# Delta-rule phase of a hybrid layer: a key copy ahead of a weight cast, two weight low halves ahead of a cell expansion, and four more projection parts before the solver's first products

## The reference

```python
u = rmsnorm(h, norm_w)
proj = einsum('btd,dc->btc', u, w_in)          # four HGRN2 kinds, four delta-rule kinds, gates
# HGRN2, 4 heads: q, forget gate f, input i, output gate z; chunked causal scan
# Gated DeltaNet, 4 heads, per chunk of tokens:
A   = beta[..., None] * einsum('bhtd,bhsd->bhts', k, k) * dec_strict
lhs = eye(C) + A
sol = triangular_solve(lhs, concat([beta * v, beta * exp(gam) * k], -1), lower=True)
u_  = sol[..., :dv] - sol[..., dv:] @ S
o   = (q * exp(gam)) @ S + (einsum('bhtd,bhsd->bhts', q, k) * dec_incl) @ u_
S   = exp(g_last) * S + (k * exp(g_last - gam)).T @ u_
out = rmsnorm(h + concat([y_hg, y_gd], -1) @ w_out, final_norm_w)[:, 16:]
```

## Time and profile before

| | us |
|---|---|
| median of three runs | 833.71 (833.3 to 834.06) |
| the profiled execution | 836.43 |
| its span from first to last instruction | 834.7 |
| PE busy in it | 730.5 (88%) |
| DVE, POOL, ACT busy | 459.0, 347.9, 313.6 |

### The profile page before, as it was taken

The page is one execution under the profiler, slowest core; times in us unless marked ns, Lnnn a source line. Parts: engine busy times, 40 slices in busy tenths (PEclk is TensorE's granted clock), DMA queues, the critical chain, the costliest instruction groups (busy, mean ns, idle before and its releaser), DMA issues. The chain is left out here.

```text
span 834.7 us, 13559 instructions
## 1 busy us (share of the span) xinstructions
PE 730.5 (88%) x4803; PEld 687.6 (82%) x4803; DVE 459.0 (55%) x1011; ACT 313.6 (38%) x788; POOL 347.9 (42%) x455
## 2 busy tenths in 40 slices
PE   3398579989999998999998999999899968999985
PEld 3377579988899998989998989899899856888764
DVE  5625333525888244478862534989335164865146
ACT  4422383144454322533543244444431322332123
POOL 3626213134655342166543231658241335845125
PEclk9599789999999999999999999999999987999989
DMA  8410604242121425580636251202252133211004
GB/s 218 51 15 3 104 8 45 44 58 26 26 35 34 56 35 67 30 49 4 39 55 47 50 65 22 31 14 37 49 131 27 59 121 120 89 45 46 0 27 201
DMA packets 77030, 45.52 MB, mean 55 GB/s; under 512 B 30894, under 2 KB 72212, under 8 KB 76964
## 3 DMA queue, kind: packets, MB, share of 16 engines
q1 hardware_dynamic: 76964, 44.66, 31.9%
HBM read 36.41 MB, written 8.24 MB: 53 GB/s over the span
## 5 line engine op out<-in xcount | busy, mean ns | idle before, releaser
L221 PE MATMUL proj<-uTh,w_high 128*128 128x352 f32 (+1 forms) x768 | 265.9, 346 | 28.6 <-ACT hg_z L264 8.9
L221 PE MATMUL proj<-uTh,w_low 128*128 128x352 f32 (+1 forms) x768 | 249.2, 324 | 0.0
L221 PE MATMUL proj<-uTl,w_high 128*128 128x352 f32 (+1 forms) x768 | 248.9, 324 | 0.0
L221 PEld LDWEIGHTS proj<-uTh,w_high 128*128 128x128 f32 x768 | 147.6, 192 | 31.5 <-issue 15.2
L221 PEld LDWEIGHTS proj<-uTl,w_high 128*128 128x128 f32 x768 | 147.7, 192 | 0.0
L221 PEld LDWEIGHTS proj<-uTh,w_low 128*128 128x128 f32 x768 | 146.8, 191 | 0.0
L239 POOL TENSOR_TENSOR w_low<-w_raw,w_high 128x256 fp32r<-128x256 f32 (+1 forms) x57 | 77.9, 1366 | 48.6 <-ACT w_high L231 48.6
L1537 PE MATMUL mix<-level_x 128*128 128x128 f32 x448 | 66.0, 281 | 8.8 <-POOL level_x L1171 3.4
L1537 PEld LDWEIGHTS mix<-level_x 128*128 128x128 f32 x448 | 61.4, 194 | 13.9 <-issue 12.5
L1179 POOL TENSOR_TENSOR f_suffix<-f_suffix,f_prefix 128x192 f32<-128x192 f32 x84 | 56.2, 669 | 22.2 <-DVE f_prefix L1366 13.8
L1376 DVE COPY_PREDICATED hg_scores<-mask_st,mix 128x384 f32<-128x384 uint8 (+1 forms) x96 | 52.0, 542 | 18.2 <-PE mix L1537 18.0
(11 more groups left out here) (310 smaller groups left out, 1390.7 us busy)
## 6 DMA issues: line engine op xcount, KB each, us to landing
w_raw<-in_w_in SPq DMA_DIRECT2D x32, 512.0 KB, 8.5
x_tile<-in_x SPq DMA_DIRECT2D x8, 512.0 KB, 8.4
w_raw<-y_scratch SPq DMA_DIRECT2D x8, 384.0 KB, 3.8
decay<-gamma_scratch SPq DMA_DIRECT2D x4, 576.0 KB, 4.2
landing<-in_w_out SPq DMA_DIRECT2D x4, 512.0 KB, 8.0
landing<-in_x SPq DMA_DIRECT2D x3, 512.0 KB, 3.3
y_scratch<-gd_y SPq DMA_DIRECT2D x6, 192.0 KB, 1.8
decay<-in_w_out SPq DMA_DIRECT2D x2, 512.0 KB, 3.8
```

Of the source, the lines that this page charges most:

```text
L221: last = pe.matmul(acc[:, 0:tw], w[j % 2][:, k, :], u[:, k, t0:t0 + tw], start=(k == 0 and i == 0), stop=(k == KT - 1 and i == 2))
```

## The change

Three edits in `phase_gd`, for all heads.

```diff
-        give(("blocks", 1), 28)
+        give(("blocks", 1), 32)
...
                 for key in order:
+                    take_low(pool, parts[key])
                     if key == ("blocks", 1):
                         pool.wait_ge(m_in, 16)
                         expand(pool, M, blk_m).then_inc(m_set, 1)
-                    take_low(pool, parts[key])
...
-                    if (s, g) == ("A1", 1):
+                    if (s, g) == ("A2", 0):
                         split_high(act, 1)
                     take_hg(act, parts[(s, g)])
```

## The result

The changed kernel takes 859.02 us (median of four runs, 855.32 to 862.47) against 833.65 us before: a ratio of 1.0307, 95% interval 1.0281 to 1.0333. That is 25.4 us slower. The direction was forecast, and so was what makes PE wait (M behind tile 4, then the lower clock); the size was not, 18.4 us, and 859.02 lies just above the stated range of 843 to 859. The profiled execution took 862.47 us with a span of 860.7, so its rows show 26.0 us more than those of before.

A forecast was written before the change was run, and what follows sets the result against it. PE was taken to bound the kernel, busy 730.5 of 834.7 us. Z later 17.2, less 7.6 behind Z, plus 8.8 for the clock makes 18.4; 833.7 + 18.4 = 852.1, called 852, range 843 to 859.

The forecast's parts named there:

- Tile 4 in the chain of M: Before Z, POOL expands M only after tile 4's load, cast and low half; Z 17.2 us later over four heads.
- the signs that were named: Expansion behind tile 4's low half; PE waits 4 to 8 us before Z; three old waits gone; clock below 1.00 behind Z.
- the end of the waits for N: In the solver before Y, four more parts on PE would cover the waits for N, 4.9 us in all.
- ACT's copies of Y were harmless: On ACT the copies of Y, held up by the wait for the load, finish inside POOL's 4.8 us: no cost.
- The clock: Stalls before Z drop PE to the lower clock, 2.2 us each, 8.8 us for four; bounds 0 and 11.2.
- The key copy: With ACT's cast moved behind it, PE's waits for the first key copy, 2.9 us in all, go; 0.7 us earlier per head.
- Low half of tile 3 ahead of the expansion: On POOL, idle 18.99 us there, the move costs nothing and the 5.5 us of PE waits at part 72 go.
- The second load: SP's load issued right behind tile 4's source delays it by 0 us, bound 2.1 a head; as rival 9%, 860.5 us.
- The pair in the earlier trace: Two loads issued 0.5 us apart landed after 8.7 and 10.3 us; 8.7 against the median 8.5 supported no delay.
- the chains from cast to Z: Cast, low half and expansion make M ready 5.9 us after tile 4's source lands, at most 5.3 in head 3.
- the four parts fewer: Behind Z, where PE bounds the phase, four parts fewer give back 1.9 us per head, 7.6 us in all.

The follow-up runs named there:

- a_pool: The changed kernel with tile 4's low half back behind the expansion of M on POOL, tile 3's still ahead: ratio 1.0060, 838.7 us.
- a_fill2: The changed kernel with unread matmuls (29, 33, 31, 15 in heads 0 to 3) filling PE's wait for M: ratio 1.0206, 850.8 us.
- a_wait: The changed kernel with POOL held back until the block solver is done before tile 3's low half: ratio 1.0188, 849.3 us.
- the mended one: The kernel a_pool_act, the changed kernel with tile 4 out of both the POOL and ACT chains: ratio 0.9855, 821.6 us.
- after_again: The changed kernel run once more with nothing altered: ratio 1.0309.
- a_pool_act: The changed kernel with tile 4's low half behind M's expansion and its cast behind ACT's copies of Y: ratio 0.9855, 821.6 us.
- b_low: The kernel before with only POOL's order changed, tile 3's low half ahead of the expansion, 28 parts kept: ratio 1.0066, 839.2 us.

## Why the prediction was wrong in size and right in kind

**Tile 4 in the chain of M: right.** Of the signs that were named one is missing, the end of the waits for N; the others are there, and a_pool takes away 20.6 us. That ACT's copies of Y were harmless was right only as long as M was later; with M free they cost PE 8.3 us of waits.

**The clock: right.** 8.8 us were priced; a_fill2 gives 8.6 by the time and 9.0 to 9.4 by the profiles.

**The key copy: right.** 2.9 us were priced, 4.0 measured alone, with an interval of 2.7 to 5.4. In the profile after, the first block transfer is issued 0.7 us earlier in its phase in head 0, as priced, and 0.9 in the others.

**The step that failed** is "Low half of tile 3 ahead of the expansion. POOL was idle 18.99 us there, so it costs nothing". POOL was idle, but DVE was not: the gap is where DVE solves the blocks, and the low half ran into one of its multiplies in every head. The four lost 1.38, 1.75, 1.39 and 1.71 us, 6.2 in all, ahead of both N and the transfers on which everything else hangs. The sum had this term at 0. It is also why the waits for N did not go: they go in a_wait. Taking the overlap away is worth 9.9 us in the changed kernel (a_wait, of which some 3 may be chance), 5.8 in the mended one and 11.4 in the kernel with the POOL edit alone. With it away the changed kernel stands at 849.3, below the 852 that the sum gave. A row of before would have warned: in head 0 the same DVE multiply of 128x384 takes 0.56 us alone and 1.66 beside a low half.

```profile
143.76 0.56 DVE L1796 TENSOR_TENSOR gd_o<-gd_xv,blk_mask 128x384 f32<-128x384 f32 x1
...
148.98 1.66 DVE L1796 TENSOR_TENSOR gd_o<-gd_xv,blk_mask 128x384 f32<-128x384 f32 x1
...
147.85 2.38 POOL L239 TENSOR_TENSOR w_low<-w_raw,w_high 128x1024 fp32r<-128x1024 f32 x1
```

Small multiplies are not spared. In a_pool the low half met two of 72x64 in head 0, 0.45 us together when alone:

```profile
158.87 2.68 DVE L1858 TENSOR_TENSOR blk_prod<-blk_inv,blk_y 72x64 f32<-72x64 f32 x2
...
158.89 2.54 POOL L239 TENSOR_TENSOR w_low<-w_raw,w_high 128x1024 fp32r<-128x1024 f32 x1 [8.99 <-ACT w_high L231]
```

In all three places the ends fit one engine waiting for the other: POOL ends at 161.43 and the two small ones at 161.55; POOL ends at 160.08 and the multiply, 1.17 us long when alone, at 161.11; POOL ends at 150.23 and the one of 0.56 at 150.64. The reduction between the multiplies, with one input, keeps its 0.68 us. The Trainium skill has this as a rule (SBUF — State Buffer, section Who interferes with whom): a DVE instruction with two inputs in SBUF contends with a GpSimd instruction that reads SBUF, and the one that started first makes the other wait. By that rule a low half costs wherever it meets one of the solver's multiplies, each of which reads two tensors, and the runs agree: every low half that ran beside the solver held one up, and with the wait none is held up.

**The second load: the bound was right, the value not.** I took 0 us for the load that follows and the profile after has 1.2 and 1.3 us in heads 0 and 2, 0.1 in heads 1 and 3, 2.7 of the 8.4 us that I had as the bound. The pair in the earlier trace rows was the wrong neighbour. That the load behind is the cause is borne out in head 2: 6.5 and 6.4 us without it, 7.4 to 8.4 with it in five profiles. In head 0 it is 7.1 to 7.9 in three of them, but 6.4 in a_wait and 6.1 in a_pool, where the second load was 0.6 us behind as well.

**The account.** Measured from the start of its phase, Z is later by 5.6, 8.7, 6.8 and 4.3 us, 25.4 in all, where the sum had 17.2. Against the 8.2 us between them stand 6.2 of multiplies, 2.7 of landings and 1.4 of one transfer in head 1, below, less 1.3, since the chains from cast to Z were shorter than estimated by 0.3 to 0.4 us each. That is 9.0, or 0.8 too much, and 0.6 of this is what the key copy gave beyond its price. Behind Z, the four parts fewer gave back 7.3 us where the sum had 7.6 (from Z to the end of the phase it is 95.0 us before and 87.7 in a_fill2, at full clock), and the lower clock took 9.4. So 25.4 - 7.3 + 9.4 = 27.5.

**What stays open.** In head 1 the store of the inverses needed 3.97 us from its issue until SP went on, against 2.54 before. It was 4.03 and 3.72 in head 1 of after_again and a_pool_act, and 2.5 or 2.6 in all other heads and kernels. I have no cause for it. Why the following load delays the one ahead of it in head 2, only at times in head 0 and not in the others was not tried either.

## What to carry to other kernels

When an instruction is moved in a list that is cut by a table, ask what the table now puts into the same step: here the number 32 took a second tile along, and an engine's stream made M wait for a load with which it has nothing to do. A gap on an engine is free only if the instruction that goes into it does not meet its neighbour: look at what VectorE does in GpSimd's gap, and for each of its instructions at whether it reads two tensors. And a stall of TensorE costs more than its length: four stalls of 4 to 8 us cost some 9 us more in clock.

## What the hardware showed that I had not expected

A multiply of 72x512 on VectorE, 1.04 to 1.18 us alone, took 2.53 to 3.23 us beside a GpSimd subtraction of 128x1024, and that subtraction 3.13 to 3.23 instead of 2.38 us where the multiply had started first. Even a pair of 72x64 multiplies went from 0.45 to 2.68 us.

Waits of TensorE of 2.18 us (a_pool), 2.27 and 3.12 us (b_low) ahead of the first Y were followed by work at the lower clock (1.2 GHz): that Y took 3.19, 3.51 and 3.48 us. Waits of 2.10 (b_low), 2.14 (a_pool_act) and 2.88 us (changed kernel) left it at 2.05 us, full speed. So the length of the wait alone does not tell.

With another load issued 0.6 us behind it, one of 512 KB that alone landed after 6.0 to 6.5 us took 7.2 to 7.9 in heads 0 and 2 of the changed kernel, 6.1 to 8.4 in the same heads of a_wait, a_pool and a_fill2, while that of head 1 stayed at 8.1 to 8.6 (8.4 alone).
